# Four output tiles of the last block: their convolution half multiplied inside the state-space stage, and x read back in two parts

## The chip, the cores and the metric

The kernel runs on one core of a Trainium2 chip. The metric is the time of one execution on the device in microseconds (us); lower is better. The core's engines work side by side: TensorE (PE) multiplies into PSUM, VectorE (DVE) and ScalarE (ACT) compute on SBUF and PSUM, GpSimd (POOL) has little to do in this part, and the queue of SyncE (SP) issues the transfers. Each engine runs its own instructions in the order in which they are written, and semaphores hold one engine back until another has got far enough.

## The reference

Two blocks over 1024 tokens of width 1024. The first (two layers of attention and feed-forward) is not touched here. The second one is this, cut to what matters:

```python
xn = rmsnorm_2(h, norm_gain[l])
proj = jnp.einsum('bld,dc->blc', xn, w_in[l])
u_ssm, z_ssm = proj[..., :512], proj[..., 512:1024]
h_conv, b_conv, c_conv, z_conv = (the next four slices of 512)
y_ssm = s5_mixer(u_ssm, ...) * jax.nn.silu(z_ssm)      # state-space scan, gelu, GLU with w_glu
y_conv = short_conv_mixer(h_conv, b_conv, c_conv, conv_w[l]) * jax.nn.silu(z_conv)
y = jnp.concatenate([y_ssm, y_conv], axis=-1)
h = h + jnp.einsum('blc,cd->bld', y, w_out[l])
return rmsnorm_2(h, final_norm_gain)
```

The output product over w_out sums over 1024 channels: 512 that come from the state-space half (y_ssm) and 512 from the convolution half (y_conv). The h that is added is itself the first block's normalised output.

## The kernel before

Activations lie transposed: 128 channels on the partitions, the 1024 tokens along the row; a "chunk" k is one such slab. A product in near-full precision is made of three fast ones: each operand is split into a rounded high part and a low part (value minus high), and `split_products` (the matmuls at L1036) multiplies high by high, high by low and low by high. For one output tile of 128 columns and four chunks that is 4 chunks x 3 products x 2 halves of the row = 24 matmuls of 128x512.

The last block's end has these stages, in PE's order:

- the product u (four steps, one for each weight tile), until 2615.5 us of the span;
- the turning of u (`u^T`, L1447), copied to `uT` by ACT and DVE in turn;
- `w re` and `w im` in two halves h (L1458), which DVE takes through `turn_back(h)` (L2561 to L2567), sixteen scans `states(h)` (L2574) and `turn_forth(h)` (L2584 to L2586), which counts `s_ready`;
- `y_near(d)` (L1467) and `y_far(d)` (L1478), summed in one accumulator, d = 0, 2 and then 1, 3; y_far waits for s_ready. `gelu` on ACT (L1859) waits for `lag_used`, which the last y_near counts; then the results are turned back (`y^T`, L1486) and copied into `yT`;
- the GLU product (L1024), whose result passes through sigmoid (L1887), `glu_ready` (L2611, L2612), `y_highs` (ACT, L1878) and `y_lows` (DVE, L2604), four times for y_ssm. The same two functions split y_conv, which has been ready for long: they do it just before the GLU product;
- eight output tiles m. `out_part(m, True)` is the convolution half and `out_part(m, False)` the state-space half of tile m, 24 matmuls each. Between them lies `x spread` (L1530), the factor of the old x as a row;
- for each tile, DVE scales x by gain and spread (L2622), adds the product (L2631) and sums the squares (L1966); ACT makes x times the final gain (L1899) and the square (L1900);
- the final norm, turned back and stored.

Three things set the order around the change. Weight tiles pass through a ring of three slots: `plan_weights` gives each tile its slot and the product after which the slot is free, and SP waits for that before it issues the load. ACT makes the high part (`tile_highs`, L1711) and DVE the low part (`tile_lows`, L2351), and PE waits for it in `tile_of`. `plan_accumulators` deals the products out to four accumulators of 128x1024 in PSUM, and PE waits in `take` until the one it needs has been read. And the memory is shared: x has no place of its own in this block. It was spilled to the output's memory, `xT` lies over `h_low_mix` and is loaded in one transfer (`x_kept`, L758) as soon as the product u is done. Output accumulators are `acc[m % 3]`.

Of the kernel before, what the change touches and what calls it, by code (L numbers as in the profile page):

```python
# [8 lines left out]
ALU = mybir.AluOpType  # L9
# [111 lines left out]
HALVES = (0, 2, 1, 3)  # L121
CONVS = [(j, w) for j in range(4) for w in range(4)]
# [30 lines left out]
def plan_accumulators():  # L153
    use = Ledger()
    def norm(n):
        use.add(("norm sum", n), 3)
        use.add(("norm spread", n), 2, frees=0)

    for k in range(KC):
        use.add(("xn", k), 2 + k % 2)  # L160
    use.block(("mix", 0), [0] * 4, [0] * 4)
    for m in range(KC):
        use.add(("wo", 0, m), m % 3)
    norm(1)
# [12 lines left out]
    use.add(("stats",), 3)  # L177
    use.add(("r spread",), 3)
    for j, w in CONVS:
        use.add(("conv", j, w), w)  # L180
        if (j, w) == (0, 3):
            use.add(("c^T",), 3)
    for what in ("win", "lag", "z", "u", "u^T"):
        for e in range(4):
            use.add((what, e), e)
    for h in range(2):
        use.add(("w re", h), 2 * h)
        use.add(("w im", h), 2 * h + 1)
# [56 lines left out]
def two_blocks_kernel(nc, x, x_rows, c, ada_tiles, columns, ffn_w_in, ffn_w_out, a_tiles, a_w_out, a_sink,  # L245
# [6 lines left out]
    with ctx:  # L252
# [268 lines left out]
        y_split = sem("y_split")  # L521
        stored = sem("stored")
# [94 lines left out]
        def _(sp):  # L617
# [389 lines left out]
        def _(pe):  # L1007
# [505 lines left out]
            def out_part(m, conv):  # L1513

                dst, ready = take(("out", m)) if conv else (acc[m % 3], acc_ready[m % 3])
                high, low = tile_of(("out", m), KC)
                shift = 0 if conv else 4
                if m == 0:
                    pe.wait_ge(y_split, 4 + shift)
                mm = split_products(dst, range(4, 8) if conv else range(4), lambda k: high[:, k, :], lambda k: low[:, k, :],  # L1520
                                    lambda k: y_high[k % 4 + shift], lambda k: y_low[k % 4 + shift], None, conv, not conv)
# [24 lines left out]
        def _(act):  # L1546
# [299 lines left out]
            tile_highs(("u", 3))  # L1846
            ready(("u", 3))
            for d in (0, 2):
                a = ready(("u", d))
                for i in range(2):  # L1850
                    ins = nc.scalar.activation(u_blk[:, 2 * d + i], a[:, HALF * i:HALF * i + HALF].rearrange("p (g h) -> p g h", g=NG),
                                               ACT.Copy, scale=r_token[:, 2 * d + i:2 * d + i + 1])
                ins.then_inc(acc_free[d], 1)
            for d in (0, 2):
# [20 lines left out]

            def y_highs(n):

                nc.scalar.activation(y_high[n], (y_conv if n < 4 else y_ssm)[:, n % 4, :], ACT.Copy).then_inc(y_high_ready, 1)  # L1878

            act.wait_ge(conv_ready, 4)  # L1880
            for e in range(4):
                y_highs(e)
            tile_highs(("out", 0))
            for e in range(4):
# [3 lines left out]
                if e == 2:  # L1888
                    tile_highs(("out", 1))
# [5 lines left out]
            tile_highs(("out", 2))  # L1895
            for m in range(KC):
# [3 lines left out]
                nc.scalar.activation(squared(6, m), xT[:, m, :], ACT.Square).then_inc(squares, 1)  # L1900
                if m + 3 < KC:
                    tile_highs(("out", m + 3))
# [8 lines left out]
        def _(dve):  # L1911
# [627 lines left out]
            tile_lows(("u", 3))  # L2539
            ready(("u", 3))  # L2540
            for d in (1, 3):
# [4 lines left out]
                ins.then_inc(acc_free[d], 1)  # L2546
            for d in (1, 3):
                copy(uT[:, 8 * d:8 * d + 8, :].rearrange("p g b -> p (g b)"), ("u^T", d))

# [39 lines left out]
            for h in range(2):  # L2589
                turn_back(h)  # L2590
                if h == 0:
# [3 lines left out]
                states(h)  # L2595
# [5 lines left out]
            def y_lows(n):  # L2601

                dve.wait_ge(y_high_ready, n + 1)
                nc.vector.tensor_tensor(y_low[n], (y_conv if n < 4 else y_ssm)[:, n % 4, :], as_f32(y_high[n]), ALU.subtract).then_inc(y_split, 1)  # L2604

            for e in range(4):
                y_lows(e)
            tile_lows(("out", 0))
            for e in range(4):
# [3 lines left out]
                if e == 2:  # L2613
                    tile_lows(("out", 1))
# [3 lines left out]
            dve.wait_ge(x_back, 48)  # L2618
            spread = ready(("x spread",)).rearrange("p (i b) -> p b i", i=TB)
            for m in range(KC):  # L2620
                x_m = xT[:, m, :].rearrange("p (b i) -> p b i", i=TB)
                ins = nc.vector.scalar_tensor_tensor(x_m, x_m, vec[:, GAINS + 32 + m:GAINS + 33 + m], spread, ALU.mult, ALU.mult)  # L2622
                if m == KC - 1:
# [4 lines left out]
                if m + 2 < KC:  # L2628
                    tile_lows(("out", m + 2))
                name = ("out", m)  # L2630
                nc.vector.tensor_tensor(xT[:, m, :], xT[:, m, :], ready(name), ALU.add).then_inc(free(name), 1)  # L2631
                sum_squares(6, m - 1)
# [56 lines left out]
```

## Time and profile before

| | |
|---|---|
| median of 3 runs | 2823.31 us (2821.97 to 2825.81) |
| the profiled execution's own time | 2823.84 us |
| its span, first to last instruction | 2821.8 us |
| PE busy | 2692.6 us (95%) |
| DVE busy | 1948.1 us (69%) |
| ACT busy | 1012.4 us (36%) |
| mean granted TensorE clock | 0.972 |

All positions below are microseconds from the start of the span. PE is busy for 95% of it, so what can be gained lies where PE stands idle or where its clock is granted at half: the granted clock is 1.00 at 2.4 GHz and 0.50 at 1.2 GHz. The shares are means over the whole span; the part of it that the change touches is the last 206 us. A matmul's printed duration overlaps its neighbours, so a run of matmuls is costed by the time from its first start to its last end.

### The profile page before, as it was taken

What the parts mean: (1) busy time and instruction counts of PE and PEld (TensorE: products, weight loads), DVE (VectorE), ACT (ScalarE), POOL (GpSimd) and SP (SyncE); (2) the same over time, 40 slices, a digit from 0 to 9 for tenths busy, and PEclk for the clock granted to TensorE, in tenths of its full rate; (3) what the DMA queues carried; (4) which work ended last, traced back from release to release, by engine and by line L of the source; (5) the groups of instructions that cost most, each with busy time, mean ns of one, the idle gap of its engine ahead of it and who ended that gap; (6) DMA issues with size and microseconds to landing.
All of it is one profiled execution on the core that took longest, in us unless ns stands there. A gap on an engine that the chain in (4) does not pass through costs nothing. (4 is left out here: it accounts for less than half of the span.)

```text
span 2821.8 us, 35472 instructions
## 1 busy us (share of the span) xinstructions
PE 2692.6 (95%) x12770; PEld 2120.5 (75%) x12770; DVE 1948.1 (69%) x3279; ACT 1012.4 (36%) x1789; POOL 271.9 (10%) x422
## 2 busy tenths in 40 slices
PE   6999699999999999999998989999999999999798
PEld 5666377788888888766675768888888878879767
DVE  6787747877778777667767597777777784331653
ACT  5554424333333332444444253333333341101232
POOL 2110000000000001101100000000000049920000
PEclk9999899999999999999998899999999999979899
DMA  5223321111111111223221111111111131121212
GB/s 225 98 98 101 138 90 53 49 52 50 55 51 52 56 48 49 97 68 98 91 82 75 34 38 57 51 56 52 48 56 52 49 113 38 45 46 32 82 38 75
DMA packets 172826, 193.08 MB, mean 68 GB/s; under 512 B 7952, under 2 KB 138224, under 8 KB 172432
## 3 DMA queue, kind: packets, MB, share of 16 engines
q1 hardware_dynamic: 160160, 147.45, 16.1%
q0 software_dynamic: 12560, 44.20, 5.1%
q8 instruction: 68, 1.11, 0.2%
q14 instruction: 38, 0.31, 0.0%
HBM read 177.86 MB, written 12.58 MB: 67 GB/s over the span
## 5 line engine op out<-in xcount | busy, mean ns | idle before, releaser
L2085 DVE SCALAR_TENSOR_TENSOR xT<-psum,mod,xT 128x1024 f32<-128x1024 f32 x352 | 446.6, 1280 | 143.0 <-PE psum L1255 143.0
L1255 PE MATMUL psum<-hT_high,w_low 128*128 128x512 f32 x1344 | 360.0, 390 | 4.1 <-DVE xT L2085 4.1
L1255 PEld LDWEIGHTS psum<-hT_high,w_low 128*128 128x128 f32 x1344 | 251.8, 188 | 58.6 <-DVE xT L2085 6.6
L1613 ACT ACTIVATE w_high<-wpair 128x512 fp32r<-128x512 f32 x294 | 184.6, 632 | 227.2 <-DMA wpair<-in_ffn_w_in_dram 129.4
L1036 PE MATMUL psum<-hT_high,w_low 128*128 128x512 f32 x944 | 260.2, 395 | 2.1 <-DVE arena L2481 2.1
L1036 PEld LDWEIGHTS psum<-hT_high,w_low 128*128 128x128 f32 x944 | 179.4, 191 | 40.5 <-DVE arena L2481 2.3
L1255 PE MATMUL psum<-h_low,w_low 128*128 128x512 f32 x672 | 207.6, 390 | 2.3 <-DVE h_low L2080 2.3
L1083 PE MATMUL psum<-hT_high,w_low 128*128 128x512 f32 x480 | 203.7, 424 | 1.9 <-DVE h_low_mix L2369 1.2
L1223 PE MATMUL psum<-hT_high,w_high 128*128 128x512 f32 x504 | 196.8, 391 | 3.5 <-DVE w_low L2045 3.5
L1732 ACT ACTIVATE arena<-arena 128x384 f32<-128x384 f32 (+3 forms) x320 | 157.7, 494 | 116.3 <-DVE arena L2266 116.3
L1224 PE MATMUL psum<-h_low,w_high 128*128 128x512 f32 x504 | 196.6, 390 | 0.0
L1225 PE MATMUL psum<-hT_high,w_low 128*128 128x512 f32 x504 | 196.4, 390 | 0.0
L1085 PE MATMUL psum<-hT_high,w_low 128*128 128x512 f32 x480 | 188.6, 393 | 0.0
L1084 PE MATMUL psum<-h_low_mix,w_low 128*128 128x512 f32 x480 | 187.8, 391 | 0.0
L2045 DVE TENSOR_TENSOR w_low<-wpair,w_high 128x512 fp32r<-128x512 f32 x252 | 172.8, 686 | 3.7
L2060 DVE TENSOR_TENSOR wpair<-wpair 128x512 f32<-128x512 f32 x168 | 115.9, 690 | 69.7 <-PE psum L1225 64.2
L1255 PEld LDWEIGHTS psum<-h_low,w_low 128*128 128x128 f32 x672 | 126.2, 188 | 29.2 <-DVE h_low L2080 3.1
L2351 DVE TENSOR_TENSOR w_low<-wpair,w_low 128x1024 fp32r<-128x1024 f32 x74 | 94.0, 1271 | 72.7 <-ACT w_low L1711 72.6
L1139 PE MATMUL psum<-arena 64*128 64x256 f32 (+3 forms) x640 | 119.8, 432 | 23.0 <-DVE arena L2260 20.8
L1083 PEld LDWEIGHTS psum<-hT_high,w_low 128*128 128x128 f32 x480 | 89.8, 187 | 64.0 <-issue 45.5
L1224 PE MATMUL psum<-hid_low,w_high 128*128 128x512 f32 x336 | 131.2, 391 | 0.0
L1631 ACT ACTIVATE hT<-hT 128x512 f32<-128x512 f32 x84 | 53.2, 633 | 168.3 <-DVE hT L2090 168.0
(340 smaller groups left out, 5261.1 us busy)
## 6 DMA issues: line engine op xcount, KB each, us to landing
wpair<-in_ffn_w_in_dram SPq DMA_DIRECT2D x176, 256.0 KB, 2.9
wpair<-in_ffn_w_out_dram SPq DMA_DIRECT2D x88, 256.0 KB, 2.8
wpair<-in_ada_tiles_dram POOLq DMA_DIRECT2D x20, 1024.0 KB, 5.4
wpair<-in_ada_tiles_dram POOLq DMA_DIRECT2D x32, 512.0 KB, 3.6
wpair<-in_w_in_dram SPq DMA_DIRECT2D x24, 512.0 KB, 3.8
wpair<-in_b_tiles_dram SPq DMA_DIRECT2D x18, 512.0 KB, 3.3
arena<-in_ada_tiles_dram SPq DMA_DIRECT2D x8, 1024.0 KB, 16.4
out_dram<-xT SPq DMA_DIRECT2D x16, 512.0 KB, 3.0
```

The costliest lines, as they stand in the source:

```text
L1036: mm = nc.tensor.matmul(dst[:, HALF * t:HALF * t + HALF], w(k), src(k)[:, HALF * t:HALF * t + HALF], start=first and n == 0 and w is high ...
L1083: nc.tensor.matmul(dst, high[:, k, :], hT_high[:, k, rows], start=k == 0, stop=False)
L1084: nc.tensor.matmul(dst, high[:, k, :], h_low_mix[:, k, rows], start=False, stop=False)
L1085: mm = nc.tensor.matmul(dst, low[:, k, :], hT_high[:, k, rows], start=False, stop=k == KC - 1)
L1223: nc.tensor.matmul(bank[dst], high[:, k, :], high_of(k), start=start and k == 0, stop=False, skip_group_check=not start)
L1224: nc.tensor.matmul(bank[dst], high[:, k, :], low_of(k), start=False, stop=False, skip_group_check=not start)
L1225: mm = nc.tensor.matmul(bank[dst], low[:, k, :], high_of(k), start=False, stop=k == 3, skip_group_check=not start)
L1255: mm = nc.tensor.matmul(dst[:, HALF * t:HALF * t + HALF], w, src[:, t, :], start=n == 0, stop=n == 2)
L1613: nc.scalar.activation(part_high[name], part_raw[name], ACT.Copy).then_inc(part_high_ready, 1)
L1732: e = nc.scalar.activation(s, s, ACT.Exp, bias=stat_n[:, ti, h:h + 1], accum_out=stat_l[:, ti, h:h + 1])
L2045: nc.vector.tensor_tensor(part_low[name], part_raw[name], as_f32(part_high[name]), ALU.subtract).then_inc(part_split, 1)
L2085: nc.vector.scalar_tensor_tensor(xT[:, m, :], acc[m % 2] if src is None else src, mod[:, l, 40 + m:41 + m], xT[:, m, :], ALU.mult, ALU.add ...
```

## The change

The convolution half of output tiles 0 to 3 is multiplied in the state-space stage as products of their own, `out conv m`, from two new weight tiles (rows of chunks 4 to 7, 256 columns each). ACT copies each result to `xT[m]`. In the tail these four tiles have only their state-space half, `out_ssm(m)`, from two weight tiles of chunks 0 to 3; tiles 4 to 7 stay whole. The tail's order becomes 4, 0, 5, 1, 2, 6, 3, 7. The high parts of y_conv are made early, in `conv_high` (in the memory of h_low_mix), and copied to `y_high` where they were before once that is free (`high_back`). x comes back in two transfers, chunks 0 to 3 into the arena (`x_early`) after the last y_far, chunks 4 to 7 into xT after high_back, and for tiles 0 to 3 DVE has one addition more. The order of the accumulators in the stage, and on DVE that of the memset of s_prev, changes with it.

```diff
+OUT_TURN = (4, 0, 5, 1, 2, 6, 3, 7)
...
     for h in range(2):
-        use.add(("w re", h), 2 * h)
-        use.add(("w im", h), 2 * h + 1)
+        use.add(("w re", h), 0)
+        use.add(("w im", h), 1)
+        for n in range(2):
+            use.add(("out conv", 2 * h + n), 2 + n)
     for what in ("y", "y^T"):
         for n, e in enumerate(HALVES):
-            use.add((what, e), n)
+            use.add((what, e), (n + 2) % 4)
...
-    for m in range(KC):
-        use.add(("out", m), m % 3)
+    for n, m in enumerate(OUT_TURN):
+        use.add(("out", m), n % 3)
...
+TILES += [(("out conv", n), ("out conv", 2 * n + 1)) for n in range(2)]
 TILES += [(("glu", n), ("glu", 2 * n + 1)) for n in range(2)]
-TILES += [(("out", m), ("out", m)) for m in range(KC)]
+TILES += [(("out", m), ("out", m)) for m in (4, 5)]
+TILES += [(("out ssm", n), ("out", 2 * n + 1)) for n in range(2)]
+TILES += [(("out", m), ("out", m)) for m in (6, 7)]
...
+        conv_high = [h_low_mix[:, 4 + e, :] for e in range(4)]
+        x_early = arena[:, 12288:16384].rearrange("p (k t) -> p k t", k=4)
...
# SP
+            for n in range(2):
+                load_tile(("out conv", n), out2_rows[:, 4:KC, 256 * n:256 * n + 256], 4)
             done, number = read_by(("u", 3))
             sp.wait_ge(done, number)
...
-            sp.dma_start(xT[:, :, :], x_kept).then_inc(x_back, 16)
             for n in range(2):
                 load_tile(("glu", n), glu_rows[:, :, 256 * n:256 * n + 256], 4)
-            for m in range(KC):
-                load_tile(("out", m), out2_rows[:, :, P * m:P * m + P], KC)
-            sp.wait_ge(x_back, 48)
+            load_out(4)
+            d, number = acc_number(("y", 3))
+            sp.wait_ge(acc_ready[d], number)
+            sp.dma_start(x_early, x_kept[:, 0:4, :]).then_inc(x_back, 16)
+            sp.wait_ge(high_back, 4)
+            sp.dma_start(xT[:, 4:KC, :], x_kept[:, 4:KC, :]).then_inc(x_back, 16)
+            load_out(5)
+            for n in range(2):
+                load_tile(("out ssm", n), out2_rows[:, 0:4, 256 * n:256 * n + 256], 4)
+            load_out(6)
+            load_out(7)
+            sp.wait_ge(x_back, 64)
# PE
+            def out_conv(m):
+                dst, ready = take(("out conv", m))
+                high, low = tile_of(("out conv", m // 2), 4)
+                cols = slice(P * (m % 2), P * (m % 2) + P)
+                split_products(dst, range(4), lambda k: high[:, k, cols], lambda k: low[:, k, cols], lambda k: conv_high[k], lambda k: y_low[k],
+                               (lambda k: pe.wait_ge(y_split, k + 1)) if m == 0 else None).then_inc(ready, 1)
...
                     mm.then_inc(ready, 1)
+                out_conv(h)
+            out_conv(2)
+            out_conv(3)
...
-            out_part(0, True)
-            out_part(1, True)
-            out_part(0, False)
+            out_part(4, True)
+            out_part(5, True)
+            out_part(4, False)
             (x spread)
-            out_part(1, False)
-            for m in range(2, KC):
-                out_part(m, True)
-                out_part(m, False)
+            out_ssm(0)
+            out_part(5, False)
+            out_ssm(1)
+            out_ssm(2)
+            out_part(6, True)
+            out_part(6, False)
+            out_ssm(3)
+            out_part(7, True)
+            out_part(7, False)
# ACT
             tile_highs(("u", 3))
+            for n in range(2):
+                tile_highs(("out conv", n))
...
+            act.wait_ge(conv_ready, 4)
+            for e in range(2):
+                y_highs(e)
             for d in (0, 2):
                 copy(uT[:, 8 * d:8 * d + 8, :].rearrange("p g b -> p (g b)"), ("u^T", d))
+                y_highs(2 + d // 2)
+            for m in range(4):
+                copy(xT[:, m, :], ("out conv", m))
...
-            act.wait_ge(conv_ready, 4)
             for e in range(4):
-                y_highs(e)
-            tile_highs(("out", 0))
+                nc.scalar.activation(y_high[e], as_f32(conv_high[e]), ACT.Copy).then_inc(high_back, 1)
+            tile_highs(("out", 4))
...
-                if m + 3 < KC:
-                    tile_highs(("out", m + 3))
+                if n in (1, 3, 4):
+                    tile_highs({1: ("out ssm", 1), 3: ("out", 6), 4: ("out", 7)}[n])
# DVE
             tile_lows(("u", 3))
+            for n in range(2):
+                tile_lows(("out conv", n))
...
+            for e in range(2):
+                y_lows(e)
             for d in (1, 3):
                 copy(uT[:, 8 * d:8 * d + 8, :].rearrange("p g b -> p (g b)"), ("u^T", d))
+            for e in range(2, 4):
+                y_lows(e)
...
                 turn_back(h)
+                states(h)
                 if h == 0:
                     ready(("w im", 1))
                     for r in range(2):
                         nc.vector.memset(s_prev[:, r, :, 0:1], 0.0)
-                states(h)
                 turn_forth(h)
...
-            for e in range(4):
-                y_lows(e)
-            tile_lows(("out", 0))
+            tile_lows(("out", 4))
...
-            dve.wait_ge(x_back, 48)
+            tile_lows(("out ssm", 0))
+            dve.wait_ge(x_back, 64)
...
+                if m < 4:
+                    copied(("out conv", m))
+                    after(nc.vector.tensor_tensor(xT[:, m, :], xT[:, m, :], x_early[:, m, :], ALU.add))
+                if n in (2, 4, 5):
+                    tile_lows({2: ("out ssm", 1), 4: ("out", 6), 5: ("out", 7)}[n])
```

## Rows read from the trace of the kernel before

**Rows 1.** Busy time by stretch: PE, PEld, DVE, ACT, POOL (instructions); clock, DMA share, GB/s.

```profile
2568.30:2615.50 47.20, 47.16 (x193) 46.85 (x192) 3.68 (x4) 3.19 (x4) 0.00 (x0) 1.00 0.07 23
...
2625.10:2648.70 23.60, 10.99 (x160) 10.59 (x160) 19.43 (x30) 0.00 (x0) 0.00 (x0) 0.86 0.27 90
2648.70:2670.80 22.10, 20.95 (x112) 20.33 (x112) 19.45 (x28) 4.01 (x4) 0.00 (x0) 0.61 0.00 0
...
2729.90:2800.80 70.90, 70.90 (x315) 58.70 (x314) 31.03 (x27) 19.79 (x19) 0.00 (x0) 1.00 0.13 36
```

**Rows 2.** The chain that ended last, by time: start us, us, what.

```profile
2628.93 1.23 DVE arena L2561
...
2633.80 1.14 DVE arena L2565
...
2648.73 13.34 PE psum L1478 x64
2662.07 5.71 PE psum L1467 x32
...
2668.88 2.01 PE psum L1486 x16
2670.89 7.01 PE psum L1478 x64
...
2711.80 16.34 PE psum L1036 x72
...
2729.93 70.77 PE psum L1036 x312
```

**Rows 3.** PE's instructions in order of time, state-space stage; idle before in brackets.

```profile
2625.08 7.21 PE L1458 MATMUL psum<-hT,arena 128*64 128x128 f32 x128 [1.41 <-DVE hT L1935]
2633.95 3.81 PE L1467 MATMUL psum<-arena,hT 128*128 128x128 f32 x32 [1.67 <-DVE arena L2564]
2648.73 13.34 PE L1478 MATMUL psum<-arena 64*128 64x128 f32 x64 [10.97 <-DVE arena L2586]
```

**Rows 4.** DVE's instructions in order of time, same stage.

```profile
2621.96 1.22 DVE L1935 COPY hT<-psum 128x1024 f32<-128x1024 f32 x1 [3.73 <-PE psum L1447]
2623.71 1.23 DVE L1935 COPY hT<-psum 128x1024 f32<-128x1024 f32 x1 [0.52 <-PE psum L1447]
...
2667.22 1.22 DVE L2586 TENSOR_TENSOR arena<-arena 128x1016 f32<-128x1016 f32 x1
```

**Rows 5.** ACT's instructions in order of time, same stage.

```profile
2615.50 2.42 ACT L1851 ACTIVATE hT<-psum,r_token 128x512 f32<-128x512 f32 x4 [30.36 <-PE psum L1433]
2620.35 1.02 ACT L1559 ACTIVATE hT<-psum 128x1024 f32<-128x1024 f32 x1 [2.43 <-PE psum L1447]
```

**Rows 6.** Lines L1878 and L2604, y_highs and y_lows: count, ns min/median/max, first and last start.

```profile
L1878 ACT ACTIVATE hT_high<-arena x8: 1042/1047/1063, 2680.8 to 2715.6; 128x1024 fp32r<-128x1024 f32 x8
...
L2604 DVE TENSOR_TENSOR hid_low<-arena,hT_high x4: 1210/1214/1218, 2682.0 to 2685.4; 128x1024 fp32r<-128x1024 f32 x4
```

**Rows 7.** PE by stretch: us, busy (instructions), granted clock, DMA share, GB/s.

```profile
2648.70:2665.50 16.80, 16.77 (x80) 0.50 0.00 0
2683.00:2687.00 4.00, 4.00 (x7) 0.57 0.00 0
```

**Rows 8.** The load of x, and loads of weight tiles after 2610: us to landing.

```profile
xT<-out_dram SPq DMA_DIRECT2D x1, 4096.0 KB, 12.2
...
DMA to landing us min/median/max: 3.8/4.1/16.6
```

**Rows 9.** DVE and ACT by line, 2729.9 to 2800.8: busy, mean ns, idle before.

```profile
L2622 DVE SCALAR_TENSOR_TENSOR xT<-xT,vec,psum 128x1024 f32<-128x1024 f32 x8 | 10.2, 1275 | 12.1 <-PE psum L1530 12.1
L2631 DVE TENSOR_TENSOR xT<-xT,psum 128x1024 f32<-128x1024 f32 x8 | 9.8, 1219 | 31.2 <-PE psum L1036 31.2
...
L1899 ACT ACTIVATE arena<-xT,vec 128x1024 f32<-128x1024 f32 x7 | 8.1, 1154 | 54.6 <-DVE xT L2631 54.6
L1711 ACT ACTIVATE w_low<-wpair 128x1024 fp32r<-128x1024 f32 x5 | 5.3, 1054 | 1.6 <-DMA wpair<-in_w_out_dram 1.6
```

More of the change, by code:

```diff
@@ L521, in two_blocks_kernel @@
         y_split = sem("y_split")
+        high_back = sem("high_back")
         stored = sem("stored")
@@ L757, in _, with load_out @@
                 sp.wait_ge(x_spilled[k], 16)
-            sp.dma_start(xT[:, :, :], x_kept).then_inc(x_back, 16)
+            def load_out(m):
+                load_tile(("out", m), out2_rows[:, :, P * m:P * m + P], KC)
             for n in range(2):
                 load_tile(("glu", n), glu_rows[:, :, 256 * n:256 * n + 256], 4)
-            for m in range(KC):
-                load_tile(("out", m), out2_rows[:, :, P * m:P * m + P], KC)
-            sp.wait_ge(x_back, 48)
+            load_out(4)
[10 more added lines that the diff above has]
+            sp.wait_ge(x_back, 64)
             for t in range(ST):
@@ L1513, in out_part @@
             def out_part(m, conv):
-                dst, ready = take(("out", m)) if conv else (acc[m % 3], acc_ready[m % 3])
+                d = OUT_TURN.index(m) % 3
+                dst, ready = take(("out", m)) if conv else (acc[d], acc_ready[d])
                 high, low = tile_of(("out", m), KC)
                 shift = 0 if conv else 4
-                if m == 0:
+                if m == OUT_TURN[0]:
                     pe.wait_ge(y_split, 4 + shift)
+                    if conv:
+                        pe.wait_ge(high_back, 4)
                 mm = split_products(dst, range(4, 8) if conv else range(4), lambda k: high[:, k, :], lambda k: low[:, k, :],
@@ L1523, in out_part, with out_ssm @@
                     mm.then_inc(ready, 1)
-            out_part(0, True)
-            out_part(1, True)
-            out_part(0, False)
+            def out_ssm(m):
+                dst, ready = take(("out", m))
+                high, low = tile_of(("out ssm", m // 2), 4)
+                cols = slice(P * (m % 2), P * (m % 2) + P)
+                split_products(dst, range(4), lambda k: high[:, k, cols], lambda k: low[:, k, cols], lambda k: y_high[4 + k],
+                               lambda k: y_low[4 + k]).then_inc(ready, 1)
+            out_part(4, True)
+            out_part(5, True)
+            out_part(4, False)
             dst, ready = take(("x spread",))
@@ L1853, in _, with y_highs @@
                 ins.then_inc(acc_free[d], 1)
+            def y_highs(n):
+                if n < 4:
+                    nc.scalar.activation(conv_high[n], y_conv[:, n, :], ACT.Copy).then_inc(y_high_ready, 1)
+                else:
+                    nc.scalar.activation(y_high[n], y_ssm[:, n - 4, :], ACT.Copy).then_inc(y_high_ready, 1)
+            act.wait_ge(conv_ready, 4)
+            for e in range(2):
+                y_highs(e)
             for d in (0, 2):
                 copy(uT[:, 8 * d:8 * d + 8, :].rearrange("p g b -> p (g b)"), ("u^T", d))
+                y_highs(2 + d // 2)
+            for m in range(4):
+                copy(xT[:, m, :], ("out conv", m))
             def gelu(d):
@@ L1888, in _ @@
                 if e == 2:
-                    tile_highs(("out", 1))
+                    tile_highs(("out", 5))
                 if e:
@@ L1894, in _ @@
             y_highs(7)
-            tile_highs(("out", 2))
-            for m in range(KC):
+            tile_highs(("out ssm", 0))
+            for n, m in enumerate(OUT_TURN):
                 copied(("out", m))
@@ L1899, in _ @@
                     nc.scalar.activation(x_gained[m], xT[:, m, :], ACT.Copy, scale=vec[:, GAINS + 48 + m:GAINS + 49 + m]).then_inc(gained_last, 1)
-                nc.scalar.activation(squared(6, m), xT[:, m, :], ACT.Square).then_inc(squares, 1)
-                if m + 3 < KC:
-                    tile_highs(("out", m + 3))
+                nc.scalar.activation(squared(6, n), xT[:, m, :], ACT.Square).then_inc(squares, 1)
+                if n in (1, 3, 4):
+                    tile_highs({1: ("out ssm", 1), 3: ("out", 6), 4: ("out", 7)}[n])
             act.wait_ge(acc_free[3], ACC[("norm sum", 6)][2] + 1)
@@ L2546, in _, with y_lows @@
                 ins.then_inc(acc_free[d], 1)
+            def y_lows(n):
+                dve.wait_ge(y_high_ready, n + 1)
+                v, high = (y_conv[:, n, :], conv_high[n]) if n < 4 else (y_ssm[:, n - 4, :], y_high[n])
+                nc.vector.tensor_tensor(y_low[n], v, as_f32(high), ALU.subtract).then_inc(y_split, 1)
+            for e in range(2):
+                y_lows(e)
             for d in (1, 3):
                 copy(uT[:, 8 * d:8 * d + 8, :].rearrange("p g b -> p (g b)"), ("u^T", d))
+            for e in range(2, 4):
+                y_lows(e)
             def full(ap):
@@ L2599, in _ @@
                 copied(("y^T", f))
-            def y_lows(n):
-                dve.wait_ge(y_high_ready, n + 1)
-                nc.vector.tensor_tensor(y_low[n], (y_conv if n < 4 else y_ssm)[:, n % 4, :], as_f32(y_high[n]), ALU.subtract).then_inc(y_split, 1)
-            for e in range(4):
-                y_lows(e)
-            tile_lows(("out", 0))
+            tile_lows(("out", 4))
             for e in range(4):
@@ L2613, in _ @@
                 if e == 2:
-                    tile_lows(("out", 1))
+                    tile_lows(("out", 5))
                 if e:
@@ L2617, in _ @@
             y_lows(7)
-            dve.wait_ge(x_back, 48)
+            tile_lows(("out ssm", 0))
+            dve.wait_ge(x_back, 64)
             spread = ready(("x spread",)).rearrange("p (i b) -> p b i", i=TB)
-            for m in range(KC):
-                x_m = xT[:, m, :].rearrange("p (b i) -> p b i", i=TB)
+            for n, m in enumerate(OUT_TURN):
+                x_m = (x_early if m < 4 else xT)[:, m, :].rearrange("p (b i) -> p b i", i=TB)
                 ins = nc.vector.scalar_tensor_tensor(x_m, x_m, vec[:, GAINS + 32 + m:GAINS + 33 + m], spread, ALU.mult, ALU.mult)
-                if m == KC - 1:
+                if n == KC - 1:
                     ins.then_inc(acc_free[3], 1)
@@ L2627, in _ @@
                     after(ins)
-                if m + 2 < KC:
-                    tile_lows(("out", m + 2))
+                if m < 4:
[3 more added lines that the diff above has]
+                    tile_lows({2: ("out ssm", 1), 4: ("out", 6), 5: ("out", 7)}[n])
                 name = ("out", m)
                 nc.vector.tensor_tensor(xT[:, m, :], xT[:, m, :], ready(name), ALU.add).then_inc(free(name), 1)
-                sum_squares(6, m - 1)
+                sum_squares(6, n - 1)
             copied(("out", KC - 1))
```

2 lines of the change are left out of this document (removed).

## The prediction, made before the run

> **What bounds the kernel now.** I read the page first (PE 95% busy), then the busy time by stretch over the last 206 us, then the chain that ended last, and last the three engines' own timelines around the stage that the change fills. The reader is to see two kinds of stretch. In the tail, from 2729.9 to 2800.8, PE is busy for all 70.90 us at a granted clock of 1.00 [rows 1]: it is the bound there, and every matmul taken away is time. The chain says what one costs: 16.34 us for 72 and 70.77 us for 312, both 0.227 us each [rows 2]. In the state-space stage it is the other way round. Between 2625.1 and 2648.7 PE is busy for 10.99 of 23.6 us while DVE is for 19.43 [rows 1]: DVE's rotations and scans run without a break from 2628.93 to 2668.44 (2667.22 + 1.22), 39.5 us [rows 2, 4]. PE waits 10.97 us for the first half's states before y_far [rows 3].
>
> That idle time costs twice. The first y_far pair takes 13.34 us where the second takes 7.01 for the same 64 instructions, and the second y_near pair 5.71 us where the first took 3.81 [rows 2, 3]. The granted clock is 0.50, the level of 1.2 GHz, from 2648.7 to 2665.5, after PE had stood idle [rows 7]. So in this stage 10.97 (idle) + 6.33 + 1.90 (half clock) + 1.67 (idle before y_near) = 20.9 us of PE's time do nothing, and the stage still ends no later than PE's own queue lets it: s_ready for the second half comes at 2668.44, and the y_far that uses it starts at 2670.89, because lag_used, gelu and the turning come first [rows 2, 4].
>
> **The change, part by part.** *Removed from the tail*: four convolution halves, 4 x 24 = 96 matmuls of 0.227 us = 21.8 us [rows 2]. All of them lie on PE's bound stretch or in the 16.34 us ahead of it.
>
> *Put into the stage*: the same 96. I lay PE's queue out anew, at full clock. w of half 0 starts at 2625.08 as before and takes half of 7.21, to 2628.8. out conv 0 takes 24 x 0.227 = 5.4, to 2634.3. w of half 1 now shares accumulators 0 and 1 with half 0, so it waits for turn_back(0) to have read them: L2564 ends at about 2633.8 and L2565 at about 2634.95 [rows 2], w re 1 starts at 2634.3 and w im 1 some 1.8 us after, so neither waits. w ends at 2637.9. Three more convolution products of 5.4 end at 2654.2. Their accumulators (2, 3, 2, 3) are freed by an ACT copy of about 1.0 us [rows 5] under the next product. y_near takes 3.81 (2658.0), y_far 7.01 (2665.1; s_ready came at 2648.7), y_near 3.81 (2668.9) [rows 2, 3]. Then lag_used comes at 2668.9, where it came at 2662.07 + 5.71 = 2667.8. Everything behind (gelu, turning, y_far, turning, GLU) keeps its order, so the GLU product starts **1.1 us later** than before. The hole was 20.9 us and 21.8 fill it; the rest is rounding and waits.
>
> *DVE in the stage*: its chain must not move. turn_back(0) waits for w im 0, which is unchanged. The memset of s_prev waits for w im 1 to have read what it overwrites; moved behind states(0) it is reached at 2641.4 by the rows' sum, after w im 1's 2637.9. Cost 0; without the move DVE would have waited from 2636.2, some 1.7 us. turn_back(1) finds w of half 1 ready. s_ready for the second half stays near 2668.4, 3.6 us ahead of the y_far that needs it at 2672: DVE has slack now.
>
> *The early split of y_conv*: four y_highs of 1.05 us on ACT and four y_lows of 1.21 on DVE [rows 6]. Two pairs are queued ahead of the u^T copies. ACT is free at 2617.9 (2615.50 + 2.42) [rows 5] and finishes two at 2620.0; its first u^T copy came at 2620.35 [rows 5]. DVE starts at 2619.0 and ends at 2621.4; its first copy came at 2621.96 [rows 4]. Cover 0.3 and 0.5 us: hidden, narrowly. Without cover both engines' pairs would push the copies, and PE's w behind them, by at most 2 x 1.21 = 2.4. The other two pairs follow the copies: DVE's second copy ends at 2624.94 [rows 4], and two y_lows later it is 2627.4, before out conv 0 starts and before turn_back(0) is due. Removed in exchange: the four y_lows before the GLU product, which were hidden under it; ACT keeps four copies there (high_back), at the same price as the y_highs they replace. Cost 0.
>
> *Four ACT copies* of out conv m to xT: ACT did nothing there but a table load (4.01 us busy in 22.1 [rows 1]). Cost 0.
>
> *Splits of out conv tiles* go under the product u, 47.2 us of PE in which DVE is busy for 3.68 and ACT for 3.19 [rows 1]. Their slots come free after u's second and third of four equal steps of 11.8, at 2591.9 and 2603.7, and a tile takes about 4.1 us to land [rows 8], so both are split before 2611. u's 3 is first in both queues, so nothing waits.
>
> *SP*: glu 1 waits for out conv 1 (2643), out 4 for out conv 3 (2654), both long before their use. Behind out 4, SP waits for the last y_far (2670.89 + 7.01 + 1.1, about 2679), then for high_back (four ACT copies after 2680.8 + 1.1, about 2686 [rows 6]), and five tile loads stand behind that. The first of them, out 5, waits for glu 1 (about 2698, halfway through the GLU product) anyway. Cost 0. x in two halves: 4 MB took 12.2 us [rows 8], so 2 MB some 6 to 7; the second lands near 2693, and x_back is wanted when x spread is done, at 2731. Slack 38 us. Before, x travelled with the glu tiles (up to 16.6 us to landing [rows 8]), which delayed nobody, so nothing is won there.
>
> *The tail*: from the GLU's end at 2711.8 + 1.1 = 2712.9 [rows 2] PE has 24 x 3 matmuls (16.34), x spread (1.78) and 13 - 3 = 9 products of 5.44 left: it would end at 2780 against 2800.70. DVE has 30 instructions from x spread on (8 scalings of 1.28, 8 additions of 1.22, 4 new additions, 3 splits, 7 sums), about 37 us of 49 [rows 9]. In total it keeps up, but the order matters: tile 6 is needed when out_ssm(2) ends, at 2752.8. Walking both queues from 2731.0: ACT handles tiles 4, 0, 5, 1 (1.15 + 1.04 each after DVE's addition [rows 9]) and makes the high part of tile 6 at 2750.8 to 2751.9; DVE, which has scaled and added for 1 and 2, makes the low part to 2753.4. PE waits **0.7 us**. Bounds: 0 if DVE is a little quicker; 2.4 if it is reached one scaling and one addition later. Tile 7's low part is made at 2759.0 and wanted at 2770. The accumulators come back in time: the closest is out 1, which needs out 4 read, at 2733.6, and starts at 2742.
>
> **The sum.** -21.8 + 1.1 + 0.7 = -20.0 us. Against the profiled execution's own 2823.84: 2803.8. The median of the runs is 0.5 us below that execution, so **2803.3 us** (-0.7%).
>
> *A rule and the rows.* y_far ran for 16.8 us at 0.50 with PE busy for 16.77 of them, and the clock came back only when y_near ran [rows 7]: these half-height (64-row) products did not bring the full clock back. The Trainium skill, "TensorE: Matmul & The Clock Gate", section "What's actually happening", says that the slow level is the default and that activity releases it; by that rule alone the busy y_far should have brought the clock back, and the trace does not agree. By the rule a PE kept busy by out conv must hold the full clock through y_far, and my sum stands; by the rows, y_far might let it go of itself, which is rival 1.
>
> **Rivals.**
>
> 1. *The half clock stays with y_far.* The first pair runs at 0.50 again, right behind the convolution products. For: the row above. Against: the second pair took 7.01 us, full clock, behind only 3.8 us of y_near. Price 6.33, or 8.2 with the y_near behind it: 2809.6 to 2811.5.
> 2. *The vector side delays w.* The y_highs and y_lows ahead of the u^T copies are not hidden. For: covers of 0.3 and 0.5 us only. Against: both covers are positive by the rows. PE is now the chain of the whole stage, so each microsecond counts fully. Price up to 2.4, and one more of 1.2 if the last y_lows holds turn_back(0): 2804.5 to 2807.
> 3. *The tail becomes DVE's.* Each of the state-space-only tiles gives PE 5.44 us of work and DVE four to five instructions of 1.2 to 1.3, 5 to 6 us. For: two of these stand back to back (1, 2). Against: tile 5's and 6's halves between them give 5.44 and 10.9 more. Price 2 to 5 us over mine: 2805.5 to 2808.
> 4. *Nothing comes out of it.* The products only displace: PE stands for them at out conv 0 (its y_split) with w of half 1 queued behind it and DVE waiting for that. It needs the last y_lows 20 us late, at 2647, though it has nothing to wait for. 2823.
> 5. *Slower*: the clock stays at 0.50 from out conv 0 to the GLU. The 51 us of PE work from 2628.8 on (21.8 convolution, 3.6 w, 7.6 y_near, 14.0 y_far, 4.3 turning) then take up to 51 more: 2854. It is slower than before from 20 us of work at half clock on. For: the clock was 0.57 at the GLU's start, so short gaps can lower it [rows 7]. Against: 312 products of just this kind ran at 1.00 in the tail [rows 1].
>
> **How the numbers follow.** Forecast 0.68, with its own range 2801 to 2806: below by tile 6 in time (-0.7) and by the half-clock stretch at the GLU's start not falling there (4 us at 0.57 cost 1.7 [rows 7]); above by tile 6 at 2.4 and a microsecond of waits. Rival 1 0.10, rival 2 0.07, rival 3 0.08, rival 4 0.04, rival 5 0.03. The range 2800.5 to 2810.5 holds the forecast, rivals 2 and 3 and half of rival 1. Faster by over 0.2% (below 2817.7; 0.2% is about what a measurement of this kernel tells from no change): 0.93. Within 0.2%: 0.04. Slower: 0.03.
>
> **What the profile after would show.** PE without a gap over 0.5 us from 2625 to 2669, clock 1.00 there; the first y_far pair in about 7 us; the GLU product ending near 2712.9 (rival 2: w later than 2625.1; rival 1: y_far 13 us). DVE's s_ready chain still ending near 2668.4. In the tail a short PE wait for w_low before tile 6 (rival 3: before several tiles). PE's last output product ending near 2780.7. The prediction is wrong if PE shows a wait for SP's tiles, for x or for conv_high, or if the split y_conv holds out conv 0.

## The result, and the profile after

The changed kernel takes 2804.47 us (median, 2802.94 to 2804.97) against 2822.64 us (2821.88 to 2825.81) for the kernel before in the same set of runs: ratio 0.9933, 95% interval 0.9915 to 0.995, so 18.2 us or 0.7% faster. The forecast was 2803.3 us. The profiled execution takes 2804.34 us and its span is 2802.3 us.

The chain that ended last, after the change; start us, us, what. It answers to [rows 2].

```profile
2623.63 3.71 PE psum L1489 x64
2627.35 5.67 PE psum L1059 x24
2633.02 3.64 PE psum L1489 x64
2636.66 16.55 PE psum L1059 x72
2653.21 3.57 PE psum L1501 x32
2656.78 7.00 PE psum L1512 x64
2663.78 3.78 PE psum L1501 x32
...
2668.66 2.01 PE psum L1520 x16
2670.67 7.01 PE psum L1512 x64
...
2682.14 29.23 PE psum L1047 x64
2711.37 16.37 PE psum L1059 x72
2727.74 1.78 PE psum L1575 x16
2729.52 16.37 PE psum L1059 x72
...
2752.20 27.46 PE psum L1059 x120
```

L1059 is the line of the split products (L1036 before), L1489 that of w, L1501 y_near, L1512 y_far, L1520 the turning of y, L1047 the GLU product. Before, the chain ran from w through DVE's rotations and scans to y_far. Now it stays on PE from 2623.63 to the last y_near. The first y_far pair takes 7.00 us where it took 13.34, the second y_near pair 3.78 where it took 5.71.

The clock says why; columns as in [rows 1], and as in [rows 7].

```profile
2627.40:2653.20 25.80, 25.80 (x162) 21.55 (x163) 25.30 (x35) 3.08 (x3) 0.00 (x0) 1.00 0.06 21
2653.20:2670.70 17.50, 16.39 (x146) 15.73 (x144) 13.58 (x24) 5.15 (x5) 0.00 (x0) 1.00 0.10 31
...
2682.00:2685.00 3.00, 2.86 (x4) 0.50 0.68 289
```

PE is busy for all of 25.80 us with the convolution products in it, and the clock is 1.00 through y_far. The stretch of half clock at the start of the GLU product is still there.

The copies that the early split of y_conv had to leave alone, on ACT and on DVE, by time:

```profile
2618.88 1.03 ACT L1609 ACTIVATE hT<-psum 128x1024 f32<-128x1024 f32 x1 [0.54 <-PE psum L1470]
...
2620.51 1.23 DVE L1995 COPY hT<-psum 128x1024 f32<-128x1024 f32 x1 [0.73 <-PE psum L1470]
...
2665.77 1.22 DVE L2659 TENSOR_TENSOR arena<-arena 128x1016 f32<-128x1016 f32 x1
```

Both still wait for PE (0.54 and 0.73 us idle), so the splits ahead of them are hidden. DVE's states for the second half are ready at 2666.99 (2665.77 + 1.22), 3.7 us before the y_far that uses them. In the tail there is one wait, with what ended it on DVE:

```profile
2752.20 0.70 PE L1059 MATMUL psum<-hT_high,w_low 128*128 128x512 f32 x2 [0.88 <-DVE w_low L2411]
```

```profile
2750.83 1.23 DVE L2411 TENSOR_TENSOR w_low<-wpair,w_low 128x1024 fp32r<-128x1024 f32 x1
```

x in two transfers, us to landing, answers to [rows 8]. They were issued at 2677.70 and 2684.47, and the second had landed 38 us before it was wanted.

```profile
arena<-out_dram SPq DMA_DIRECT2D x1, 2048.0 KB, 7.3
xT<-out_dram SPq DMA_DIRECT2D x1, 2048.0 KB, 7.4
```

**How to compare profiles here.** The changes here touch little ahead of the stage (the loads and splits of the two out conv tiles, under the product u), yet the stage began anywhere from 2609.6 to 2617.7 us, and two profiles of one and the same kernel, that with both edits, began it 6.0 us apart. At the other end SP waits for the last store:

```profile
SPq L252 <- DMA out_dram<-arena: 3.8, 1, 3.8
```

```profile
SPq L258 <- DMA out_dram<-arena: 5.2, 1, 5.2
```

The first is the kernel before, the second the changed one; over the fourteen profiles behind this text it was 3.8 to 4.2 in eight and 5.0 to 5.2 in six. The kernel with both edits shows 5.2 in one profile and 3.8 in the other, so it does not belong to the kernel. Each profile is therefore measured from its own start of the stage, the first copy of u out of PSUM on DVE (L2544 before), to two points: the start of the GLU product and the end of the last output product.

| kernel | stage starts | to GLU start | to last output product's end | median; kernel before beside it |
|---|---|---|---|---|
| before | 2615.50 | 66.85 | 185.20 | |
| changed | 2614.03 | 68.11 | 165.63 | 2804.47; 2822.64 |
| changed, a later set of runs | 2617.61 | 68.09 | 165.58 | 2805.64; 2824.83 |
| gaps filled, nothing moved | 2613.86 | 64.56 | 182.78 | 2821.34; 2824.90 |
| three products in the stage | 2617.12 | 64.58 | 162.29 | 2803.76; 2824.90 |
| two | 2614.54 | 72.23 | 171.10 | 2810.08; 2824.90 |
| five | 2614.66 | 73.54 | 171.25 | 2810.99; 2824.90 |
| memset back | 2615.63 | 68.14 | 165.69 | 2805.12; 2824.54 |
| tile 6 split earlier | 2617.65 | 68.13 | 164.61 | 2806.36; 2824.54 |
| fifth half before the GLU | 2615.48, 2616.57 | 71.30, 71.32 | 161.65, 161.66 | 2800.63; 2824.54, and 2802.83; 2824.83 |
| both | 2615.62, 2609.64 | 71.35, 71.33 | 160.56, 160.54 | 2800.91; 2824.54, and 2799.19; 2824.83 |
| both, dense spare products | 2614.70 | 71.35 | 160.55 | 2799.72; 2824.83 |

Three kernels were profiled twice, in separate sets of runs, and each gives the same figure within 0.05 us, where their medians moved by 1.2 to 2.2 us. The change is worth 185.20 - 165.63 = 19.6 us by it. Taken against the kernel before beside it, each median agrees with its mark within 2.4 us; the worst is tile 6 split earlier, 18.2 us by the medians and 20.6 by the mark. So differences of 1 us below stand on the marks alone.

### The profile page after: what moved, and what is told of

Its sections match the earlier page's. It is cut to its first block and busy times, and to the rows that moved or that the text cites. A ratio compares the mean times of both kernels' runs of the same rounds, so it can differ in the third digit from the quotient of the medians.

```text
span 2802.3 us, 35494 instructions
## 1 busy us (share of the span) xinstructions
PE 2684.2 (96%) x12770; PEld 2111.9 (75%) x12770; DVE 1951.9 (70%) x3283; ACT 1020.1 (36%) x1797; POOL 271.6 (10%) x422
## 5 line engine op out<-in xcount | busy, mean ns | idle before, releaser
L1278 PE MATMUL psum<-hT_high,w_low 128*128 128x512 f32 x1344 | 360.0, 390 | 4.1 <-DVE xT L2145 4.0
L1278 PEld LDWEIGHTS psum<-hT_high,w_low 128*128 128x128 f32 x1344 | 251.8, 188 | 58.6 <-DVE xT L2145 6.6
L1059 PE MATMUL psum<-hT_high,w_low 128*128 128x512 f32 x880 | 243.4, 395 | 3.0 <-DVE arena L2541 2.1
L1106 PE MATMUL psum<-hT_high,w_low 128*128 128x512 f32 x480 | 203.7, 424 | 2.4 <-DVE h_low_mix L2429 1.7
L1059 PEld LDWEIGHTS psum<-hT_high,w_low 128*128 128x128 f32 x880 | 167.4, 191 | 39.3 <-DVE arena L2541 2.3
L1248 PE MATMUL psum<-hT_high,w_low 128*128 128x512 f32 x504 | 196.5, 390 | 0.0
L1108 PE MATMUL psum<-hT_high,w_low 128*128 128x512 f32 x480 | 188.5, 393 | 0.0
L1106 PEld LDWEIGHTS psum<-hT_high,w_low 128*128 128x128 f32 x480 | 89.9, 187 | 64.3 <-issue 45.5
L1761 ACT ACTIVATE w_low<-wpair 128x1024 fp32r<-128x1024 f32 x74 | 78.0, 1054 | 112.2 <-DMA wpair<-in_w_in_dram 79.6
```

The costliest lines, as they stand in the source:

```text
L1059: mm = nc.tensor.matmul(dst[:, HALF * t:HALF * t + HALF], w(k), src(k)[:, HALF * t:HALF * t + HALF], start=first and n == 0 and w is high ...
L1106: nc.tensor.matmul(dst, high[:, k, :], hT_high[:, k, rows], start=k == 0, stop=False)
L1108: mm = nc.tensor.matmul(dst, low[:, k, :], hT_high[:, k, rows], start=False, stop=k == KC - 1)
L1248: mm = nc.tensor.matmul(bank[dst], low[:, k, :], high_of(k), start=False, stop=k == 3, skip_group_check=not start)
L1278: mm = nc.tensor.matmul(dst[:, HALF * t:HALF * t + HALF], w, src[:, t, :], start=n == 0, stop=n == 2)
```

## The experiments

**What the clock alone is worth** (gaps filled). The kernel before with PE's two waits for s_ready filled with products that add a constant to the y accumulators:

```diff
+            fill(22, acc[0][:, 0:256])      # matmul(dst, ident, pick[:, 0:2, :], start=False, stop=False)
             pe.wait_ge(s_ready, 2)
             for d in (0, 2):
                 y_far(d)
...
+            fill(11, acc[2][:, 0:256])
             pe.wait_ge(s_ready, 4)
```

> The kernel before, nothing moved, but PE's two waits for s_ready filled with 22 and 11 products of the identity (about 0.45 us each) added onto the y accumulators, so the output has a constant added to it. It asks what the restored clock alone is worth. Hole theory (mine): y_far's first pair falls from 13.3 to about 7 us and y_near's second from 5.7 to 3.8, but the second half's states come at 2668.4 all the same, so y_far's second pair starts at most 2.4 us earlier: total -2.4 us. Clock theory (rival): the half clock itself cost the stage its 8.2 us and their return is a large part of the change's gain: total about -8 us.

Its PE by time:

```profile
2647.13 7.07 PE L1478 MATMUL psum<-arena 64*128 64x128 f32 x64 [1.47 <-DVE arena L2593]
2654.13 3.84 PE L1467 MATMUL psum<-arena,hT 128*128 128x128 f32 x32
...
2660.93 4.92 PE L1495 MATMUL psum<-pick,ident 128*128 128x256 f32 x22
2666.89 7.07 PE L1478 MATMUL psum<-arena 64*128 64x128 f32 x64 [1.04 <-DVE arena L2593]
```

y_far and y_near run at full clock, yet the GLU product starts only 66.85 - 64.56 = 2.3 us earlier: the second y_far waits for DVE (L2593, turn_forth). The ratio to the kernel before was 0.9989 (0.9979 to 0.9998). The 8.2 us that the half clock had added here were mostly waiting in another form: what PE no longer spends on slow products it spends waiting for DVE. They are worth something once other work takes their place.

**Three and two products in the stage.** The changed kernel with out conv 3, or 2 and 3, cut to 2 matmuls each; 22 and 44 are left out, and these tiles lack that part of their sum:

```diff
                 cols = slice(P * (m % 2), P * (m % 2) + P)
+                if m >= 3:        # 2 in the second kernel
+                    for t in range(2):
+                        mm = nc.tensor.matmul(dst[:, HALF * t:HALF * t + HALF], high[:, 0, cols], conv_high[0][:, HALF * t:HALF * t + HALF], start=True, stop=True)
+                    mm.then_inc(ready, 1)
+                    return
```

> The changed kernel with the convolution product of tile 3 cut to 2 of its 24 matmuls (22 are left out, 5.0 us of PE). Hole theory: s_ready for the second half (2667.0) now bounds y_far's second pair, which started at 2670.7, so the GLU product starts 3.6 us earlier, not 5.0: total -3.6 us. Rival, PE alone bounds the stage: -5.0 us.

> The changed kernel with the convolution products of tiles 2 and 3 cut to 2 matmuls each (44 left out, 10.0 us of PE). Hole theory: nothing more is won over the run with only tile 3 cut, since DVE's states set the start of y_far's second pair: total -3.6 us against the changed kernel if the clock stays at 1.00. PE now stands idle for some 5 us before that pair; if the clock falls to 0.50 in that wait, the pair takes up to 13.3 instead of 7 us and the total is +2.7. Rival, PE alone bounds the stage: -10.0 us.

With three the GLU product starts 68.11 - 64.58 = 3.5 us earlier, though 5.0 us of work are gone. The number is that of the kernel with the gaps filled (64.56): DVE's chain is the floor of this stage. The second y_far pair, which waits for DVE in all three, starts 53.03 us into the stage with the gaps filled, 53.05 with three products and 53.02 with two, so less work on PE does not bring it below. With two the GLU product starts 4.1 us later than in the changed kernel, not earlier. PE by time, and by stretch:

```profile
2660.65 2.01 PE L1525 MATMUL psum<-ident,hT 128*128 128x128 f32 x16 [1.11 <-ACT hT L1930]
2667.56 13.34 PE L1517 MATMUL psum<-arena 64*128 64x128 f32 x64 [4.90 <-DVE arena L2664]
2680.82 3.67 PE L1525 MATMUL psum<-ident,hT 128*128 128x128 f32 x16
```

```profile
2660.00:2667.50 7.50, 2.01 (x16) 0.84 0.00 0
2667.50:2681.00 13.50, 13.44 (x65) 0.50 0.00 0
2681.00:2684.60 3.60, 3.50 (x16) 0.50 0.80 269
```

PE had less to do, stood idle for 4.90 us before y_far, the clock fell, and y_far ran its whole 13.34 us at 0.50. The expectation said +2.7 us in that case; the turning behind it ran at half clock too (3.67 us for 2.28) and so did the start of the GLU product, so it was +4.1 at the GLU and +5.5 at the last output product. That the idle time did it is read from the run with three products, where PE waited 0.37 us for the same states and y_far took 7.08 us.

**Five products.** The changed kernel with the product of tile 3 done twice:

```diff
+                if m == 3:
+                    split_products(dst, range(4), lambda k: high[:, k, cols], lambda k: low[:, k, cols], lambda k: conv_high[k], lambda k: y_low[k])
                 split_products(dst, range(4), ...
```

> The changed kernel with the convolution product of tile 3 done twice (24 matmuls more, same result). Hole theory: the hole is full with four, so the fifth product costs its whole 5.4 us in the stage: +5.4 us. Rival, there is still room (the stage lost only 1.3 us to four products): +1 to +2 us.

The GLU product starts 5.4 us later (73.54 against 68.11). The four products fill what was there. Against the stage with its gaps filled (64.56) the first three together cost nothing (the run with three still has 2 matmuls of the fourth), the fourth costs 3.5 and a fifth its full 5.4.

**The memset.** The changed kernel with the memset of s_prev back ahead of states(0):

```diff
                 turn_back(h)
-                states(h)
                 if h == 0:
                     ready(("w im", 1))
                     for r in range(2):
                         nc.vector.memset(s_prev[:, r, :, 0:1], 0.0)
+                states(h)
```

> The changed kernel with the memset of s_prev back ahead of states(0), so that DVE waits for w im 1 before its scans. Theory: w im 1 ends at 2636.7 and DVE gets there at 2634.8, so its chain slips by 1.9 us; PE's y_far pairs start 9.5 and 3.6 us after their states, so the total does not move (within 0.3 us). Rival, DVE's chain still bounds the stage: +1.9 us.

DVE by time:

```profile
2638.45 0.07 DVE L2667 MEMSET arena<- 128x16 f32 x1 [2.07 <-PE psum L1489]
```

DVE waits 2.07 us for w im 1, its chain ends 2.0 us later, and the GLU starts at 68.14 against 68.11: nothing. The move protects a chain that has 3.7 us of slack.

**Tile 6 split one tile earlier.**

```diff
-                if n in (1, 3, 4):                     # ACT, tile_highs: ssm 1, 6, 7
+                if n in (1, 2, 4):
...
-                if n in (2, 4, 5):                     # DVE, tile_lows: ssm 1, 6, 7
+                if n in (2, 3, 5):
```

> The changed kernel with weight tile 6 split one output tile earlier on ACT and DVE. Theory: PE's wait of 0.9 us for w_low before tile 6 goes: -0.9 us. Rival, the wait moves to another tile or accumulator: 0.

The last output product ends 1.0 us earlier (165.63 to 164.61); the chain has one piece of 216 matmuls where the wait was:

```profile
2733.25 49.01 PE psum L1059 x216
```

**The fifth half before the GLU product.** Accumulators and the order on PE; the splits of tile 4 move up on ACT and DVE, and the second load of x waits for the new semaphore too:

```diff
+    use.add(("out", OUT_TURN[0]), 2)
     for e in range(4):
-        use.add(("glu", e), e)
+        use.add(("glu", e), (0, 1, 3, 0)[e])
-    for n, m in enumerate(OUT_TURN):
+    for n, m in enumerate(OUT_TURN[1:]):
         use.add(("out", m), n % 3)
...
+            dst, _ = take(("out", 4))        # before the GLU product
+            high, low = tile_of(("out", 4), KC)
+            split_products(dst, range(4, 8), lambda k: high[:, k, :], lambda k: low[:, k, :], lambda k: conv_high[k % 4],
+                           lambda k: y_low[k % 4], None, True, False).then_inc(conv_read, 1)
...
-            out_part(4, True)
             out_part(5, True)
-            out_part(4, False)
             (x spread)
+            out_part(4, False)
```

> The changed kernel with the convolution half of tile 4 multiplied between the last turning of y and the GLU product, where PE waits 2.26 us for DVE's copy; the GLU's accumulators are 0, 1, 3, 0 and tile 4 keeps accumulator 2. Theory: PE is the bound from there to the last output product, so what is won is the wait filled (2.3 us) and the stretch of half clock at the GLU's start (1.6 us): -3.9 us. Rival 1, the clock falls there anyway, since it falls after the small-product stretch and not because of the wait: -2.3. Rival 2, the GLU's chain to y_split is late by the 3.1 us that the product sticks out of the wait, and that shows in the tail: 0 or above.

The last output product ends 4.0 us earlier (165.63 to 161.65). The chain by time, then PE by stretch in the later profile of the same kernel:

```profile
2681.31 5.47 PE psum L1062 x24
2686.78 27.51 PE psum L1050 x64
```

```profile
2685.00:2688.00 3.00, 3.00 (x14) 1.00 0.56 240
2688.00:2692.00 4.00, 4.00 (x10) 1.00 0.76 266
```

The GLU product takes 27.51 us instead of 29.23: with the wait of 2.3 us filled the clock no longer falls. It ends 3.2 - 1.7 = 1.5 us later than before, and the tail has 5.5 us less to do.

**Both, and against each other on one chip.**

> The two edits of the runs with tile 6 split earlier and with the fifth convolution half before the GLU, together. Theory: they add up, -4.8 us against the changed kernel, about 2799.7 us.

> The kernel with both edits (tile 6 earlier, fifth convolution half before the GLU), and the eight spare products at the last norm (4.5 us from the last output product to the norm's matmuls, 3.6 of them busy) replaced by 19 of the dense 128x512 kind that fill the wait. In two of the earlier profiles with tile 6 split early, and in one with the convolution product doubled, the clock was 0.50 for 3 to 7 us in the store's turnings, in the others not. Theory: PE's light stretch at the norm lets the clock fall in some executions; with it filled densely it falls in none, the turnings take 7.1 us always, and the median is 1 to 2 us under that of the kernel with both edits, with less spread. Rival, the norm's own small matmuls and the turnings let it fall whatever stands ahead of them: no difference.

> The kernel with both edits again, beside the others on one chip. Theory: -5.1 us against the changed kernel from the stage's start to the last output product, as in its first profile; in the median some of that is taken back by the half clock at the store: -3 to -5.

> The kernel with the fifth convolution half before the GLU alone, again. Theory: -4.0 us against the changed kernel.

> The changed kernel again, on the same chip as the last three, so that they can be compared with it: 19 to 20 us under the kernel before. From the start of u's copies to the last output product 165.6 us, as in its first profile.

The edit of the run with dense spare products, at the last norm:

```diff
+                if n == 6:
+                    high, _ = tile_of(("out", 7), KC)
+                    for i in range(19):
+                        nc.tensor.matmul(psum[:, 3584:4096], high[:, i % 4, :], y_high[4 + i % 4][:, 0:HALF], start=True, stop=True)
+                else:
+                    spare_products(8, ...)
```

| kernel, one chip | median us | lowest to highest | ratio to before (95%) |
|---|---|---|---|
| before | 2824.83 | 2819.21 to 2831.63 | |
| changed | 2805.64 | 2803.70 to 2809.89 | 0.9930 (0.9916 to 0.9944) |
| fifth half before the GLU | 2802.83 | 2801.05 to 2805.55 | 0.9921 (0.9906 to 0.9936) |
| both edits | 2799.19 | 2794.25 to 2803.28 | 0.9911 (0.9896 to 0.9927) |
| both, dense spare products | 2799.72 | 2794.36 to 2804.04 | 0.9909 (0.9893 to 0.9924) |

By the marks both edits together give 165.6 - 160.55 = 5.0 us in both profiles, 4.8 were expected; the medians give 2805.64 - 2799.19 = 6.4. The fifth half alone gives 4.0 by the marks, as expected, and 2.8 by the medians. The kernel with both edits has the lowest median in this table, and its range does not overlap that of the changed kernel, though it does that of the fifth half alone. In the set of runs before this one, the earlier split of tile 6 had shown nothing in the medians: 2806.36 with it against 2805.12 for the kernel with the memset back, which is the changed kernel by its marks, and 2800.91 with both edits against 2800.63 with the fifth half alone (kernel before: 2824.54). In the profiles of these two kernels with tile 6 split earlier the turnings of the store had run partly at half clock, 9.96 us and 8.72 us for 64, where the kernels they were compared with have 7.06:

```profile
2788.92 9.96 PE psum L1591 x64
```

That is not peculiar to the earlier split: the turnings took 9.92 us with five products and 8.44 with two. The dense spare products were to prevent it. In their one profile the turnings took 7.06 us, but median and spread are those of the kernel with both edits. And the fastest execution of all those profiled, 2794.25 us with both edits, has turnings of 8.72 us; against the other profile of the same kernel (2801.80 us) its stage began 6.0 us earlier and its last store's wait was 1.4 us shorter, which is nearly all of the difference. So the theory that this fall decides the median is not borne out, and it is open whether the dense products prevent the fall.

## Why the prediction was right

*The bound.* The tail was PE's and the 96 matmuls taken from it were time: 19.6 us net by the profiles, 20.0 forecast.

*The stage.* "The GLU product starts 1.1 us later" measured 1.26. PE's queue as laid out held piece by piece: w starts 9.6 us into the stage as before, w of half 1 follows out conv 0 without a wait, y_near, y_far and y_near take 3.57, 7.00 and 3.78. Two small errors of the sum offset each other in part. Added without its roundings its pieces give 0.9 and not 1.1. The measured pieces are longer by 0.4 for the convolution products, which stand here between products of another kind (out conv 0 takes 5.67 us and not 5.44, the three behind it 16.55 and not 16.34), by 0.1 for w, and shorter by 0.24 for the first y_near (3.57, not 3.81).

*The half clock.* The forecast rested on its return. Rival 1 (y_far lets the clock go of itself) did not happen: 7.00 us at 1.00. The run with two products shows what does it here, an idle wait of 4.90 us ahead of it, and that y_far then does not bring it back: PE was busy for 13.44 of 13.50 us at 0.50. By the Trainium skill's rule ("TensorE: Matmul & The Clock Gate", "What's actually happening") that activity releases the slow level it should have come back, and the trace disagrees a second time. The prediction misread one row: of the 16.8 us in [rows 7] y_far has only the first 13.4, the last 3.4 are the y_near behind it, still at 0.50. And it laid the low clock on the products of 64 rows, which stays open: with two products the turnings behind y_far, of 128 rows, stayed at 0.50 as well (busy 3.50 of 3.60 us).

*DVE and SP.* Rival 2 did not happen; the copies waited for PE by 0.54 and 0.73 us where the sum left 0.3 and 0.5. The cost given for leaving the memset where it was (1.7 us of DVE's time) measured 2.07, and it is nothing in the total. The 16.6 us to landing that the prediction gave to the glu tiles [rows 8] were those of the first output tile; the two glu tiles beside x took 14.5 in the median.

*The tail.* One wait, at tile 6, as the two queues had been walked: 0.88 us where 0.7 was forecast. Rival 3 did not come: the kernel has no other wait for w_low. Rivals 4 and 5 did not either: out conv 0 started right behind w, and the clock was 1.00 from 2627.40 to 2670.70.

*The total.* The two terms mis-sized are small, 1.1 for 1.26 and 0.7 for 0.88. With them the sum is -19.66, and the marks give -19.57. The profiled executions differ by 19.5 us: 19.6 in the stage and the tail, 1.5 from an earlier start of the stage, and 1.5 back behind the last output product, of which 1.4 is the last store's wait. The start varies as much without the change, and so does the store's wait; that the two cancel is luck. In the later set of runs the median moved by 19.2 us.

*What the forecast did not say* is how near the change stands to a cliff. With one product less the stage would be at DVE's floor, and with two less the clock falls.

## What to carry to other kernels

An idle hole on the busiest engine is worth what else can be put into it, not what its half clock seems to cost: with the clock alone restored this stage won 2.3 of 8.2 us, because the other engine's chain was right behind. Fill such a hole as long as a piece costs less there than it saves elsewhere: here each product saves 5.4 us in the tail, the first three cost nothing in the stage, the fourth 3.5 and a fifth its full 5.4 us, so that a fifth in this place would win nothing. Before the GLU product it won 4.0, because there it also filled a wait and the clock stayed up. Where the starts of a stage vary by 8 us from run to run, a change of 1 to 5 us is read from marks inside the profile, from the stage's own start on.

## What the runs showed of the hardware that was not expected

Taking work away made the kernel slower: with two products instead of three PE idled for 4.90 us, and the last output product ended 8.8 us later (171.10 against 162.29). The products of 64-row operands (y_far) ran for 13.4 us at half clock without bringing the full clock back. In the kernel before it came back while the y_near behind them ran, after 3.4 us of it at 0.50; with two products it had not come back after 3.50 us of turnings. A second case stands earlier in the kernel before: other products of 64-row operands kept PE busy from 2499.6 to 2523.4 at 0.50, and the clock was still 0.50 up to 2526, in the first 128x512 products behind them. No run swaps the kind of product alone. A wait of 2.3 us after a stretch of small products was enough for 1.7 us lost at the GLU product's start, and none was lost with the wait filled. The last store's wait was 3.8 to 4.2 or 5.0 to 5.2 us, in two profiles of one kernel once each; what decides that was not tried.
